# The products of a recurrent walk on TensorE: one 128x128 product for two heads, or one 64x64 tile a head

## The reference

```
def step(S, inp):
    r_t, w_t, k_t, v_t, a_t, b_t = inp
    sa = jnp.einsum('bhij,bhj->bhi', S, a_t)
    S = S * w_t[:, :, None, :] + sa[..., None] * b_t[:, :, None, :] + v_t[..., None] * k_t[:, :, None, :]
    return S, jnp.einsum('bhij,bhj->bhi', S, r_t)
```

## Time and profile before

| what | value |
|---|---|
| three runs | 2915.48, 2919.69, 2932.57 us; median 2919.69 |
| span of the profiled execution | 2934.0 us |
| PE busy in it | 2523.1 us, 86% |
| DVE, POOL, ACT busy | 1629.7, 1466.9, 966.9 us |
| stretch with walks | 611 to 1538 us after the span's start |

### The profile page before, as it was taken

One profiled execution on the slowest core, in us unless ns is written; L12 is line 12 of the kernel. 1 busy time (PEld: TensorE's weight loads), 2 busy tenths in 40 slices (PEclk: granted clock), 3 DMA queues, 4 the chain that ended last, 5 costly groups with the idle time before them and its releaser, 6 DMA issues.

```text
span 2934.0 us, 45044 instructions
## 1 busy us (share of the span) xinstructions
PE 2523.1 (86%) x15926; PEld 2170.6 (74%) x15926; DVE 1629.7 (56%) x2297; ACT 966.9 (33%) x2235; POOL 1466.9 (50%) x907
## 2 busy tenths in 40 slices
PE   6799999898888878888888589999998689978876
PEld 5789899787887777887778589566667667666555
DVE  6766666676666676666754453133332427347755
ACT  1532323354454444544432122223231111121331
POOL 1466656554434444444547568022208678775334
PEclk8899999798999989999898789999998889989998
DMA  2243343611222112321122112100001322121101
GB/s 85 92 152 151 138 153 142 165 30 41 65 53 45 41 41 54 64 45 41 41 94 74 50 64 87 43 30 29 29 29 51 103 65 86 50 71 58 44 0 57
DMA packets 141815, 201.95 MB, mean 69 GB/s; under 512 B 101888, under 2 KB 104064, under 8 KB 139392
## 3 DMA queue, kind: packets, MB, share of 16 engines
q1 hardware_dynamic: 141696, 200.20, 22.5%
HBM read 161.18 MB, written 38.99 MB: 68 GB/s over the span
## 4 chain that ended last, share of the span: by engine, by line
PE 72%; DVE 16%; issue 6%; ACT 3%; POOL 1%; DVEq 0%; DMA 0%; SPq 0%; ACTq 0%; POOLq 0%
PE wide L1182 10%; PE wide L1183 10%; PE wide L1184 10%; PE wide L770 8%; PE wide L775 5%; PE wide L1665 4%; PE wide L355 4%; PE wide L1760 2%; PE wide L1725 2%; PE wide L1724 2%; DVE w_rounded L967 2%; PE wide L751 1%; PE wide L757 1%; PE wide L761 1%; PE wide L1550 1%
## 5 line engine op out<-in xcount | busy, mean ns | idle before, releaser
L1049 POOL TENSOR_TENSOR n_levels<-n,masks 128x384 fp32r<-128x384 f32 x192 | 200.2, 1071 | 179.2 <-PE wide L770 179.2
L1182 PE MATMUL wide<-mixed_high,w_high_rwkv_in 128*128 128x264 f32 x720 | 212.4, 295 | 28.9 <-ACT log_decay L435 20.0
L1184 PE MATMUL wide<-mixed_high,w_low_rwkv_in 128*128 128x264 f32 x720 | 207.1, 288 | 0.0
L1299 DVE TENSOR_TENSOR sq_sum<-sq_sum,squares 128x528 f32<-128x528 f32 (+1 forms) x54 | 86.9, 1610 | 183.5 <-ACT squares L1264 183.5
L1183 PE MATMUL wide<-u_low_second,w_high 128*128 128x512 f32 x464 | 186.3, 402 | 0.0
L1206 POOL TENSOR_TENSOR w_high<-weights,con 128x1024 fp32r<-128x1024 f32 x60 | 147.3, 2454 | 76.0 <-PE wide L1184 66.1
L958 DVE TENSOR_TENSOR w_rounded<-wide,w_rounded 128x384 fp32r<-128x384 f32 x240 | 124.8, 551 | 99.2 <-PE wide L770 98.6
L355 PE MATMUL wide<-mixed_in,weights 128*128 128x264 f32 x672 | 159.4, 396 | 13.1 <-DVE mixed_in L325 12.3
L1182 PEld LDWEIGHTS wide<-mixed_high,w_high_rwkv_in 128*128 128x128 f32 x720 | 138.5, 192 | 37.1 <-ACT log_decay L435 26.3
L1209 POOL TENSOR_TENSOR w_low<-weights,w_high 128x1024 fp32r<-128x1024 f32 x60 | 157.7, 2629 | 4.7
L355 PEld LDWEIGHTS wide<-mixed_in,weights 128*128 128x128 f32 x672 | 129.5, 194 | 40.4 <-issue 9.5
(11 more groups left out here) (350 smaller groups left out, 7913.4 us busy)
## 6 DMA issues: line engine op xcount, KB each, us to landing
weights<-in_stream SPq DMA_DIRECT2D x200, 512.0 KB, 3.5
forms<-form SPq DMA_DIRECT2D x16, 2020.5 KB, 6.3
a_r<-forms SPq DMA_DIRECT2D x16, 576.0 KB, 5.0
gate_bonus<-forms SPq DMA_DIRECT2D x16, 576.0 KB, 4.0
b_diag<-forms SPq DMA_DIRECT2D x32, 144.0 KB, 5.3
k_diag<-forms SPq DMA_DIRECT2D x32, 144.0 KB, 5.2
v_diag<-forms SPq DMA_DIRECT2D x32, 144.0 KB, 4.8
a_diag<-forms SPq DMA_DIRECT2D x32, 144.0 KB, 4.5
```

The source lines that it names most:

```text
L1049: pool.tensor_tensor(n_lvl[:, lv % LEVEL_BUFS, grp(g), :], n_all[:, grp(g), :], mask("levels", lv + 1), ALU.mult).then_inc(q["n_level"], 1)
L1182: pe.matmul(dst, w[0], x[0], start=start, stop=False)
L1184: return pe.matmul(dst, w[1], x[0], start=False, stop=stop)
```

## The change

Each of the seven products is issued as two, one for each head, on the 64x64 block of that head: rows 0 to 63 with columns 0 to 63, then rows 64 to 127 with columns 64 to 127. The off-diagonal blocks of the result in PSUM are no longer written in the walk. The semaphores for `u`, the state and the outputs become two each, one for a head's last product (`u_mm`, `s_mm`, `y_mm` are now pairs), and every engine that waited for one waits for both. After a wait of the walk TensorE executes an increment of a semaphore nobody waits for (`walk_turn`, `begin`), which takes the wait that the first product had.

```diff
-                    mm = pe.matmul(chunk_bank[:, 0:P], w_inv[:, c, :], mv[:, c, :], start=True, stop=c == 0)
+                        begin()
+                    by_head(chunk_bank, w_inv[:, c, :], mv[:, c, :], True, c == 0, u_mm if c == 0 else None)
                     if c > 0:
                         pe.wait_ge(q["s_rows"], 9 * p + c)
-                        mm = pe.matmul(chunk_bank[:, 0:P], a_hat[:, c, :], state[:], start=False, stop=True)
-                    mm.then_inc(q["u_mm"], 1)
-
-                    pe.matmul(state_bank[:, 0:P], tokens_of[:, pw, 1, c, :], v, start=True, stop=False)
+                        begin()
+                        by_head(chunk_bank, a_hat[:, c, :], state, False, True, u_mm)
+
+                    by_head(state_bank, tokens_of[:, pw, 1, c, :], v, True, False)
                     if c > 0:
                         pe.wait_ge(q["y_rows"], 9 * p + c)
-                        pe.matmul(y_bank[:, 0:P], b_r[:, pw, c, :], state[:], start=True, stop=False)
-                    pe.matmul(y_bank[:, 0:P], mg[:, pw, c, 1, :], v, start=c == 0, stop=False)
+                        begin()
+                        by_head(y_bank, b_r[:, pw, c, :], state, True, False)
+                    by_head(y_bank, mg[:, pw, c, 1, :], v, c == 0, False)
                 else:
 
                     pe.wait_ge(q["u_rows"], 9 * p + c + 1)
-                    pe.matmul(state_bank[:, 0:P], tokens_of[:, pw, 0, c, :], u_row[:], start=False, stop=True).then_inc(q["s_mm"], 1)
-                    pe.matmul(y_bank[:, 0:P], qg[:, pw, c, 1, :], u_row[:], start=False, stop=True).then_inc(q["y_mm"], 1)
+                    begin()
+                    by_head(state_bank, tokens_of[:, pw, 0, c, :], u_row, False, True, s_mm)
+                    by_head(y_bank, qg[:, pw, c, 1, :], u_row, False, True, y_mm)
+
+            def by_head(out, lhsT, rhs, start, stop, done=None):
+
+                for hd, rows in enumerate(HEAD_ROWS):
+                    cols = slice(hd * C, (hd + 1) * C)
+                    mm = pe.matmul(out[rows, cols], lhsT[rows, cols], rhs[rows, cols], start=start, stop=stop)
+                    if done:
+                        mm.then_inc(done[hd], 1)
+
+            def begin():
+
+                pe.sem_inc(q["walk_turn"], 1)
...
-                    act.wait_ge(q["u_mm"], 9 * p + c + 1)
+                    for done in u_mm:
+                        act.wait_ge(done, 9 * p + c + 1)
...
-                    dve.wait_ge(q["s_mm"], 9 * p + c + 1)
+                    for done in s_mm:
+                        dve.wait_ge(done, 9 * p + c + 1)
```

More of the change, by code:

```diff
@@ L629, in program @@
                    "u_mm", "u_rows", "s_mm", "s_rows", "y_mm", "y_rows", "g_mm", "k_mm", "post", "y_rooted", "y_turned", "z_sum",
-                   "z_made", "z_stored", "diag_set", "early_set", "late_set")
+                   "z_made", "z_stored", "diag_set", "early_set", "late_set", "u_mm_other", "s_mm_other", "y_mm_other", "walk_turn")
         sb_ = {n: sem("b_" + n) for n in b_names}
         q = sb_
+        u_mm, s_mm, y_mm = ((q[n], q[n + "_other"]) for n in ("u_mm", "s_mm", "y_mm"))
         HEAD_ROWS = (slice(0, C), slice(C, P))
@@ L672, in sp_scan @@
             if post:
-                sp.wait_ge(q["y_mm"], 9 * (i - 1))
+                for done in y_mm:
+                    sp.wait_ge(done, 9 * (i - 1))
                 sp.wait_ge(q["s_rows"], 9 * (i - 1))
@@ L871, in walk @@
                 if part == 0:
-                    act.wait_ge(q["u_mm"], 9 * p + c + 1)
+                    for done in u_mm:
+                        act.wait_ge(done, 9 * p + c + 1)
                     act.activation(u_row[:], chunk_bank[:, 0:P], ACT.Copy).then_inc(q["u_rows"], 1)
                 else:
-                    act.wait_ge(q["y_mm"], 9 * p + c + 1)
+                    for done in y_mm:
+                        act.wait_ge(done, 9 * p + c + 1)
                     if c == 0 and not is0(p):
@@ L1495, in pool_c @@
             pool.wait_ge(mixed_loaded, 16 * STORED)
-            pool.wait_ge(q["y_mm"], NC * STORED + NC)
+            for done in y_mm:
+                pool.wait_ge(done, NC * STORED + NC)
             pool.wait_ge(q["s_rows"], NC * STORED + NC)
@@ L1499, in pool_c @@
                 pool_split_tile(pool, z_t[:, k, :], y_hi[:, k, :], z_low_of(k))
-            pool.wait_ge(q["y_mm"], NC * PAIRS)
+            for done in y_mm:
+                pool.wait_ge(done, NC * PAIRS)
             pool.wait_ge(q["s_rows"], NC * PAIRS)
```

## The result

| | before | after |
|---|---|---|
| median of the runs, us | 2926.13 (4 runs, 2915.48 to 2933.47) | 3112.01 (4 runs, 3097.41 to 3118.99) |
| ratio | | 1.0626 [1.0587, 1.0664] |
| span of the profiled execution | 2934.0 | 3117.2 |
| mean granted clock of TensorE | 0.923 | 0.847 |

The account below looks back on a forecast made before the run. TensorE's own throughput was taken to bound the 25.6 us full-clock walk: 2.6 us saved a pass less 0.5 of waits, fifteen passes 31.5, pass 16 1.6; 2919.7 - 33 = 2887 us, range 2856 to 2945.

Parts of the forecast that it names:

- low-clock part: First 7.8 us of a looped walk, at 1.2 GHz; no higher saving counted there, as post items wait for DVE.
- Rival D: TensorE stays longer at 1.2 GHz because of more gaps: 7.8 us more a pass, 58 us in all, 2945; chance 0.08.
- Side by side: Both heads' walk products overlap in full on two row halves: a pair costs 0.107 us for 0.223, saving 0.116.
- rival A: The heads' walk products run one after the other because both write one PSUM bank: 68 us slower, 2988; chance 0.11.
- The change of shape: Entering and leaving the 64x64 shape costs each walk item 0.34 us, taken as 0.25 net.
- the two 0.05: Deductions per walk item: the first walk product's extra time, and the place held by the last rounded matmul before it.
- E: Rival: the switches of shape are cheap, 3.5 to 4.5 us saved a pass, 2852 to 2867; chance 0.08.
- Waits that are late next: TensorE waits on DVE's `w_rounded` adds, 0.4 us a pass, and on `s_rows` or `y_rows`, 0.1.
- rival B: Holds at `begin` stop TensorE's stream: 26 a pass at 0.08 us eat the gain, 2915 to 2922; chance 0.12.
- Pass 16: Last pass, no levels beside its walk: a chunk takes 1.65 us for 1.83, saving 1.6 us in all.
- Setup and ending: The last 26 us of a looped pass, without a walk, were to stay at 26 us.

Follow-up runs that it names:

- wide_moving: The changed kernel with each head's 64-row weights meeting all 128 moving columns, so streams stay full length; 3030.1 us, 1.0356 of the kernel before.
- last_only: The changed kernel with only the last product of each walk item tiled, 18 of 61 a pass; 3013.3 us, 1.0299 of the kernel before.
- holds_only: The kernel before, without tiles, plus the increment behind each wait of the walk, 26 a pass; 2954.1 us, 1.0097 of the kernel before.
- incs_free: The kernel before plus the same 26 increments a pass, each behind the product that keeps its wait; 2944.7 us, 1.0052 of the kernel before.
- late6: The changed kernel with tiles only from the fourth chunk on, six of nine chunks; 2902.8 us, 0.9934 of the kernel before.

## Why the prediction was wrong

**The step that failed** is the clock. The prediction cuts a pass into 7.8 us at 1.2 GHz and 25.6 at 2.4, says of the first "I don't count the low-clock part higher", and keeps this split for the changed kernel. It doesn't keep: with walk products of full length the clock is back within 9.9 us, and the change halves the stream of these products just there. In seven passes of 14 the walk stays at the low clock for all its 50.4 us, in the others for 19.4 us at least, where none had more than 9.9. 174 of the 183 us by which the span grew stand in this one place.

**Rival D** had this outcome at 0.08 and its size far too small: 7.8 us more at 0.50, 3.9 us a pass. Measured are 33 us more at 0.50 and 12.4 us a walk. It was also given its cause wrongly ("With more gaps") and its argument against ("the MLA stage has the same changes of shape and 0.98") answered that cause alone. The argument is right as far as it goes: 18 changes of shape a pass keep the clock down for some 4 us more (wide_moving, last_only), in part because the clock, once back, falls again. But the MLA stage has streams of up to 264 columns and was no witness for halved ones. The question to ask was what brings the clock back in the earlier trace rows, beside what might lower it. The sign that it named for D, a stretch at 0.50 of over 8 us in a walk, came; it was drawn from one pass, though, and the kernel before passes it too, with 9.8 or 9.9 us in three walks.

**Side by side** (against rival A): right. What the earlier trace rows show holds for one PSUM bank too. A product of two heads takes 0.11 to 0.12 us for the forecast 0.107. The Trainium skill (TensorEngine Tiling (Array Packing), Gotcha 1: PSUM Pressure) says that different row tiles cannot access the same PSUM bank at once; the trace disagrees for tiles that write different partition halves of it, where heads in turn would have needed 0.21.

**The change of shape**: the gross price was nearly right, 0.34 forecast, 0.30 to 0.33 measured (last_only); wide_moving, where products stream as before, pays 0.26. The 0.25 net was not: the two 0.05 "come off" by the forecast, and they don't. The level product ahead of a walk item holds 0.09 more, not less, and part 0 of before took 1.03 to the next level product's start, not 1.16, since that start lies beside its end. 18 x 0.08 = 1.4 us a walk was counted that isn't there. With 0.33 an item a walk saves 61 x 0.116 - 18 x 0.33 = 1.1 us; pass 1 shows 1.5. Of the 2.1 a pass forecast, half to seven tenths would have come at an unchanged clock, 17 to 23 us in fifteen passes for 31.5. By this alone the time would have been about 2900, at the slow end of the forecast's own range; E is out.

**Waits that are late next**: not seen. Six chunks save 0.9 to 1.2 us, and 42 x 0.116 - 12 x 0.33 = 0.9 leaves nothing for the 0.5 that I took off.

**Holds** (rival B): free where they were priced, in the walk (holds_only). Not free in a place that the prediction didn't look at: with 26 of them a pass, 3.0 to 3.4 us in the mean of the seven ends of a turn. In the changed kernel the rest there has grown by 2.4 us, 17 in all; what part of it is the increments isn't shown.

**Pass 16**: 0.4 us less, where 1.6 was forecast. It can't be read: kernels without any tile have 22.8 and 24.4 us there (incs_free, holds_only), and the low parts differ: the changed kernel spends 19.5 of its 23.9 us at 1.2 GHz, the kernel before 6.4 of 24.3. late6, with 21.5, is under all of these.

**Setup and ending** "stay at 26 us": right without a turn of the loop (26.3), wrong with one (31.0 for 28.7).

## What to carry to other kernels

A saving on a busy TensorE is worth what it is at the clock of before only if the work under which the clock came back stays; look in the profile at what runs between the fall of the clock and its return, and keep that work whole. Here tiles in four chunks ahead of the return cost 3.3%, and in five behind it they gain 0.6%, so a shorter stream belongs where the clock is already full. And before a cause is ruled out by a stage that has it and a full clock, see whether that stage has the other things that the change brings, the length of the streams above all.

## What the runs showed of the hardware

- A TensorE that is busy isn't enough for the full clock. In the 50.4 us walk it is busy for 48.7 us and granted 0.50 throughout. With the same items at streams of full length the clock is back 2.3 to 9.9 us into the walk; with tiles of 64 rows and full streams (wide_moving) 10.4 us of a walk are low in the mean.
- Under the same tiled items with levels between them, the clock kept its level for long. The walk that starts at 2.4 GHz stays there for all its 26 us (pass 1), those that start at 1.2 GHz stay for 19 us or more, in seven of 14 for all 50. So what is measured of such a code in one pass doesn't tell of the next. It isn't so without the levels: in pass 16 the tiled walk starts at 2.4 GHz too and falls to 1.2 after 4.4 us, where the walk of before falls after 17.9.
- A clock that has just come back can go again: in last_only it fell after 3.4 us in which TensorE was busy for 1.56, and stayed down for 17.1 us of a TensorE busy throughout.
- Two tiles of 64x64 on different row halves, and two of 128x64 on different column halves, ran side by side into one PSUM bank, loads and matmuls both: inside an item 0.11 to 0.12 us a float32 product of 64 columns.
- 26 increments a pass that nobody waits for cost 3.5 us where the loop jumps back (incs_free), and 18 with 42 tiles cost nothing (late6). The gaps there go with fetches of instructions; the cause isn't shown.
